# Down bias of all experts entered once, in the first pair's scatter, and a scatter that takes four banks in turn

## The chip, the cores and the metric

The kernel runs on one core of one Trainium2 chip. The metric is the device time of one execution in microseconds (us). Five engines matter here: TensorE (PE, with its weight loads listed apart as PEld), VectorE (DVE), ScalarE (ACT), GpSimd (POOL), and SyncE (SP), whose queue issues nearly all DMA transfers. The weights lie in HBM, the working memory is SBUF (`arena` in the profile), and TensorE writes its products to eight PSUM banks of 128 partitions x 512 float32 each.

## The reference, cut to what matters

One layer of a streaming encoder: RMSNorm, an input projection, two kinds of attention, an output projection, and then a mixture of 32 experts of which each token takes 4. 384 tokens (256 prompt rows, 128 sample rows) go through the experts. All is float32. The part that the change touches:

```python
logits = x2 @ w_router + b_router
top_val, top_idx = lax.top_k(logits, 4)
gates = softmax(top_val)
# for each expert e, for the tokens that chose it
hcat = x2[ids] @ w_gu[e] + b_gu[e]               # 1024 -> 2048
glu  = minimum(hcat[:, 0::2], 7)
lin  = clip(hcat[:, 1::2], -7, 7)
act  = glu * sigmoid(1.702 * glu) * (lin + 1)
out  = act @ w_dn[e] + b_dn[e]                   # 1024 -> 1024
y[token] += out * gate
```

The sum over experts of gate times `b_dn[e]` is linear in the bias, so it equals the matrix product of the gates (384 x 32, zero where an expert was not chosen) with `b_down` (32 x 1024).

## The kernel before, in words

The first 310 us hold norms, projections, attention, the router and the first gather. The rest is the experts, in 16 pairs (`pair`, called by `run_pairs` with `main`). The two experts of a pair have 64 slots each, so 128 rows together; expert 0 of a pair owns rows 0 to 63 and expert 1 rows 64 to 127. An expert's weights are read from HBM once, in pieces of 2 MB: a pair has 12 pieces, 8 of gate and up weights and 4 of down weights. They go through a ring of 8 buffers in SBUF. SP issues the load of a piece as soon as TensorE has done the piece that lay in its buffer (`refill`, line 575, waiting for `piece_done`); for the pieces numbered 8, 9, 16, 17, 28 and 29 it goes by halves (line 589). All pieces go in one order that is written out by hand.

TensorE's order within a pair:

1. Gate and up products (line 1943), 64 instructions of 64 columns by 512 to banks 0 to 3, with four products of 32 rows for the bias `b_gate_up` after the first eight (line 1929). They wait for their pieces.
2. If there is a next pair: its gather (line 1912), 24 products of 128 x 128 to banks 6 and 7, which ACT and DVE copy out (lines 1039 and 1444).
3. Two products of 32 rows that put the pair's `b_down` rows into banks 0 and 1 (line 1957, with `own_e`, a table of which row belongs to which expert, and `bdn2`, in which the left half of `b_down` lies on partitions 0 to 31 and the right half on 32 to 63). They wait until DVE has made two of the four parts of `act`, which empties banks 0 and 1. In the last pair a filler product follows (`keep_busy`, line 1788).
4. A wait for the six additions of the pair before (`y_added`), a wait for the last part of `act`, then eight transposes of `act` to banks 4 and 5 (line 1963) and three of the gated selection to bank 3 (line 1969).
5. Down products (line 1996; in the last pair also 1982) onto the bias in banks 0 and 1.
6. The scatter (line 2013): six products of 128 x 128 by 128 x 512, each adding its part of the pair's rows to a third of the tokens and half of the columns. It uses banks 4 and 5 in turn, and product n (from 2 on) waits for the addition of product n-2, which DVE does (line 1489). In the last pair six banks are used and nothing is waited for.

DVE makes the activation in four parts (lines 1471 to 1473 and 1459, with ACT's sigmoid at line 1045), then copies the next gather, the transposed activation and the result. `Y_BASE` and `at_` only turn counts into semaphore values. `GT` is the table of gates, 128 tokens x 32 experts for each of three groups of tokens; it is there since the router.

Of the kernel before, what the change touches and what calls it, by code (L numbers as in the profile page):

```python
# [91 lines left out]
def build(nc, io, out):  # L92
    ctx = ExitStack()
    with ctx:
# [108 lines left out]
        EG = at3(a0 + 12288 + 3 * P, E, TOPK)  # L203
        bgu4 = at(hn0, 512)
        bdn2 = at(hn0 + 512, 512)
        RK = at3(lf0, 3, E)
        GT = at3(lf0 + 96, 3, E)
        M = at3(lf0 + 192, 3, E)
# [141 lines left out]

        def scat_bank(n, last_one):

            return banks[(4, 5, 6, 7, 2, 3)[n] if last_one else 4 + n % 2]

        def turned_row(k):

# [433 lines left out]
        def _(ac):  # L790
# [248 lines left out]
                    nc.scalar.activation(XT[u][:, k], banks[6][:, P * k:P * (k + 1)], ACT.Copy,  # L1039
                                         scale=gcol_x[:, k:k + 1]).then_inc(xg_a, 1)  # L1040

            def pair(at_, u, next_at=None):
                for n in range(4):
                    ac.wait_ge(glu_ready, at_(4, n + 1))
                    nc.scalar.activation(sg[n % 2], tg[n % 2], ACT.Sigmoid, scale=1.702).then_inc(sig_ready, 1)  # L1045
                if next_at:
                    gathered(next_at, 1 - u)
                ac.wait_ge(actT_done, at_(2, 1))
                nc.scalar.activation(actT[:, 0:4], banks[4].rearrange("p (c s) -> p c s", c=4), ACT.Copy).then_inc(actT_a, 1)
                ac.wait_ge(selT_done, at_(1, 1))  # L1050
                nc.scalar.activation(gT, banks[3][:, 0:384], ACT.Copy).then_inc(selT_copied, 1)
                ac.wait_ge(down_done, at_(1, 1))
                nc.scalar.activation(rows[:, 0:512], banks[0], ACT.Copy).then_inc(rows_a, 1)  # L1053
# [1 line left out]
            ac.wait_ge(s_gx, 16)  # L1055
            gathered(lambda k, c: c, 0)
            gates(2)
            run_pairs(ac, lambda it, u, at_, nx: pair(at_, u, nx))

            def over(p, r, at_):  # L1060
                gathered(at_, 0)
# [449 lines left out]
        def _(pe):  # L1511
# [402 lines left out]
                    if k % 4 == 3:  # L1914
                        last.then_inc(xg_done, 1)

            def pair(at_, u, arrived, next_at=None, last_one=False, early=None):
                steps = [(k, n) for k in range(6) for n in range(4)]
                steps += [(6, 0), (6, 1), (7, 0), (7, 1), (6, 2), (7, 2), (6, 3), (7, 3)] if last_one else [(k, n) for n in range(4) for k in (6, 7)]
                slots_of = {}  # L1920
                for k, n in steps:
                    if (k, n) == (0, 0):
                        pe.wait_ge(xg_a, at_(4, 1))
                    if (k, n) == (1, 0):
                        pe.wait_ge(own_ready, at_(1, 1))
                        pe.wait_ge(s_bgu, 64)
                        for n_ in range(4):
                            grp = slice(E * n_, E * (n_ + 1))
                            mm(banks[n_], own_e[u][grp], bgu4[grp], start=False, stop=False, skip_group_check=True)  # L1929
                        pe.wait_ge(xg_a, at_(4, 4))  # L1930
                    if (k, n) == (4, 0):
                        pe.wait_ge(xg_v, at_(1, 1))
                    both = last_one and k >= 6
                    if both:
                        if n == 0:
                            slots_of[k] = arrived(k)
                        s = [slots_of[k]] * 2
                    elif k % 2 == 0 and n == 0:
                        s = [arrived(k + x) for x in range(2)]
                    for x in range(2):  # L1940
                        half = slice(SLOTS * x, SLOTS * (x + 1))
                        c0 = 2 * FF * (x if both else k % 2) + 512 * n
                        last = mm(banks[n][half], XT[u][:, k, half], piece_slot(s[x])[:, c0:c0 + 512],  # L1943
                                  start=(k == 0), stop=(k == 7), skip_group_check=True)
                        if n == 3 and (x == 1 if both else k % 2 == 1):
                            last.then_inc(piece_done, 1)
                        if (k, n) == (0, 3) and early == 0:
                            last.then_inc(half_done, 1)
                    if n < 3 and k == 7:
                        last.then_inc(h_done, 1)  # L1950
                if next_at:
                    gather(next_at, 1 - u)
                pe.wait_ge(act_ready, at_(4, 2))
                pe.wait_ge(s_bdn, 32)
                for hf in range(2):
                    grp = slice(E * hf, E * (hf + 1))
                    mm(banks[hf], own_e[u][grp], bdn2[grp], start=True, stop=False, skip_group_check=True)  # L1957
                if last_one:
                    keep_busy(banks[7], 512)
                pe.wait_ge(y_added, at_(6, Y_BASE))  # L1960
                pe.wait_ge(act_ready, at_(4, 4))
                for c in range(8):
                    last = nc.tensor.transpose(banks[4 + c // 4][:, P * (c % 4):P * (c % 4 + 1)],  # L1963
                                               act[:, P * c:P * (c + 1)], ident)
                    if c % 4 == 3:
                        last.then_inc(actT_done, 1)
                pe.wait_ge(selg_ready, at_(1, 1))
                for t in range(3):
                    last = nc.tensor.transpose(banks[3][:, P * t:P * (t + 1)], selg[u][:, t], ident)
                last.then_inc(selT_done, 1)  # L1970
                pe.wait_ge(actT_a, at_(1, 1))
                for i in range(3 if last_one else 2):
                    if i == 1:
                        pe.wait_ge(actT_v, at_(1, 1))
                    if last_one and i >= 1:
                        s = arrived(9 + i)
                        for hf in range(2):
                            for c in (2 * i - 2, 2 * i - 1):
                                for x in range(2):
                                    half = slice(SLOTS * x, SLOTS * (x + 1))  # L1980
                                    c0 = PIECE_W // 2 * x + D * (c % 2) + 512 * hf
                                    last = mm(banks[hf][half], actT[:, 4 + c, half], piece_slot(s)[:, c0:c0 + 512],
                                              start=False, stop=(c == 3), skip_group_check=True)
                            if i == 2 and hf == 0:
                                last.then_inc(down_done, 1)
                        last.then_inc(piece_done, 1)
                        continue
                    s = [arrived(8 + 2 * i + x) for x in range(2)]
                    order = [(hf, c) for hf in range(2) for c in range(4)]
                    if early is not None and i == 0:  # L1990
                        order = [(hf, c) for c in range(4) for hf in range(2)]
                    for hf, c in order:
                            for x in range(2):
                                half = slice(SLOTS * x, SLOTS * (x + 1))
                                w = piece_slot(s[x])[:, D * c + 512 * hf:D * c + 512 * (hf + 1)]
                                last = mm(banks[hf][half], actT[:, 4 * i + c, half], w, start=False,  # L1996
                                          stop=(i == 1 and c == 3), skip_group_check=True)
                                if (hf, c) == (1, 3):
                                    last.then_inc(piece_done, 1)
                                if early is not None and i == 0 and (hf, c) == (1, 1):  # L2000
                                    last.then_inc(half_done, 1)
                            if i == 1 and (hf, c) == (0, 3):
                                last.then_inc(down_done, 1)
                pe.wait_ge(selT_copied, at_(1, 1))
                for n in range(6):
                    t, hf = n // 2, n % 2
                    if n == 0:
                        pe.wait_ge(rows_a, at_(1, 1))
                    elif n == 1:
                        pe.wait_ge(rows_v, at_(1, 1))  # L2010
                    elif not last_one:
                        pe.wait_ge(y_added, at_(6, Y_BASE + n - 1))
                    mm(scat_bank(n, last_one), gT[:, P * t:P * (t + 1)], rows[:, 512 * hf:512 * hf + 512],  # L2013
                       start=True, stop=True).then_inc(scat_done, 1)

            def main(it, u, at_, nx):
                def arrived(r):
# [2 lines left out]
                    n = q if isinstance(it, int) and it == 0 else PIECES * PAIRS  # L2020
                    pe.wait_ge(ring_in[s], it * (16 * 3) + (16 * (q // RING + 1) + halved_in(s, n)))
                    return s
                pair(at_, u, arrived, nx, nx is None, early=u if isinstance(it, int) and it == 0 else None)

            run_pairs(pe, main, first_apart=True)

# [42 lines left out]
```

## Time and profile before

| | |
|---|---|
| runs shown | 1238.6, 1239.01, 1240.78 us; median 1239.01 us |
| span of the profiled execution | 1237.8 us |
| that execution's own device time | not listed apart; the span lies 1.2 us under the median |
| TensorE busy | 1205.1 us, 97% |
| VectorE, ScalarE, GpSimd busy | 350.3, 194.6, 158.6 us |
| mean granted TensorE clock | 0.996 |
| read from HBM | 442.00 MB |

The span runs from the first to the last instruction. "Busy" for TensorE holds the modelled time of pipelined products, so 97% does not say that it works at its peak. The clock is the share of full speed that was granted. The page cuts the span into 40 slices and gives the busy share of every engine in tenths for each.

### The profile page before, as it was taken

The page shows a single profiled execution, that of the slowest core. Times are in us where ns is not written, and L with a number is a line of the kernel's source. Part 1 is how long each engine was busy: PE and PEld are TensorE (multiplying, and loading weights), DVE is VectorE, ACT ScalarE, POOL GpSimd, SP SyncE. Part 2 cuts the span into 40 slices and gives each one's busy share as a digit, 9 for nine tenths or more (in the row PEclk, how much of TensorE's full clock was granted, in tenths as well). Part 3 has the DMA queues.
Part 4 walks back from the last instruction along what each step waited for, and adds up shares of the span by engine and source line. Part 5 has one row for each costly group of instructions (what it writes and reads, how often), then busy time and mean ns, then how long its engine had stood idle before and what let it go on. Part 6 is the DMA issues. An engine that isn't in the chain of part 4 may idle for free.

```text
span 1237.8 us, 16172 instructions
## 1 busy us (share of the span) xinstructions
PE 1205.1 (97%) x6101; PEld 525.3 (42%) x6102; DVE 350.3 (28%) x932; ACT 194.6 (16%) x519; POOL 158.6 (13%) x378
## 2 busy tenths in 40 slices
PE   9999999999999999999999999999999999999997
PEld 5444456646344343434343443434343434342433
DVE  3234366614322121213131222212121212131313
ACT  4211365513100010101010000101010101010100
POOL 0032312101320202012020202020202011020000
PEclk9999999999999999999999999999999999999999
DMA  9622343792999999999999999999999999999995
GB/s 299 258 67 98 139 138 141 272 406 94 387 425 421 426 427 427 427 428 430 428 429 427 428 430 426 430 427 430 428 428 430 426 430 426 429 430 426 428 425 225
DMA packets 57119, 448.66 MB, mean 362 GB/s; under 512 B 10594, under 2 KB 12019, under 8 KB 31219
## 3 DMA queue, kind: packets, MB, share of 16 engines
q1 hardware_dynamic: 57032, 448.05, 87.7%
q8 instruction: 29, 0.48, 0.2%
q14 instruction: 16, 0.12, 0.0%
q10 hardware_dynamic: 42, 0.01, 0.0%
HBM read 442.00 MB, written 4.86 MB: 361 GB/s over the span
## 4 chain that ended last, share of the span: by engine, by line
PE 75%; DMA 21%; DVE 2%; issue 1%; ACT 0%; SPq 0%; POOL 0%; DVEq 0%; POOLq 0%
DMA arena<-in_w_gate_up 21%; PE psum L1943 21%; PE psum L1996 17%; PE psum L1673 10%; PE psum L1912 7%; PE psum L1798 3%; PE psum L2013 3%; PE psum L1957 1%; PE psum L1963 1%; PE psum L1777 1%; PE psum L1709 1%; PE psum L1632 1%; PE psum L1929 1%; PE psum L1739 1%; PE psum L1623 1%
## 5 line engine op out<-in xcount | busy, mean ns | idle before, releaser
L1943 PE MATMUL psum<-arena 128*64 128x512 f32 x2048 | 451.9, 598 | 16.4 <-DMA arena<-in_w_gate_up 16.4
L1943 PEld LDWEIGHTS psum<-arena 128*64 128x64 f32 x2048 | 148.3, 138 | 315.4 <-issue 315.0
L1996 PE MATMUL psum<-arena 128*64 128x512 f32 x992 | 216.4, 594 | 0.7
L1471 DVE TENSOR_SCALAR arena<-psum 128x256 f32<-128x256 f32 x64 | 26.7, 418 | 394.3 <-PE psum L1943 394.3
L1996 PEld LDWEIGHTS psum<-arena 128*64 128x64 f32 x992 | 75.5, 137 | 130.7 <-issue 128.9
L1673 PE MATMUL psum<-arena 128*128 128x512 f32 x288 | 127.3, 595 | 1.4 <-DVE arena L1108 1.4
L1045 ACT ACTIVATE arena<-arena 128x256 f32<-128x256 f32 x64 | 26.7, 417 | 591.8 <-DVE arena L1471 591.8
L2013 PE MATMUL psum<-arena 128*128 128x512 f32 x192 | 92.8, 622 | 0.0
L743 POOL COPY arena<-arena 128x6 f32 (+1 forms) x16 | 3.0, 188 | 696.7 <-PE psum L1996 693.1
L1912 PEld LDWEIGHTS psum<-arena 128*128 128x128 f32 x720 | 81.5, 192 | 12.2 <-issue 12.2
L1912 PE MATMUL psum<-arena 128*128 128x128 f32 x720 | 84.4, 276 | 0.0
L1673 PEld LDWEIGHTS psum<-arena 128*128 128x128 f32 x288 | 53.4, 190 | 64.5 <-issue 62.5
L1489 DVE TENSOR_TENSOR arena<-psum,arena 128x512 f32<-128x512 f32 x96 | 66.5, 692 | 24.9 <-PE psum L2013 24.9
L1484 DVE COPY arena<-psum 128x512 f32<-128x512 f32 x16 | 11.1, 692 | 217.9 <-PE psum L1996 204.3
L2013 PEld LDWEIGHTS psum<-arena 128*128 128x128 f32 x192 | 28.9, 188 | 63.7 <-DVE arena L1489 39.5
L760 POOL TENSOR_SCALAR arena<-arena 128x64 f32<-128x64 f32 x96 | 53.9, 579 | 0.0
L1798 PE MATMUL psum<-arena 128*128 128x512 f32 x96 | 43.6, 599 | 1.0 <-DVE arena L1356 1.0
L1459 DVE TENSOR_TENSOR arena<-arena 128x256 f32<-128x256 f32 x64 | 36.4, 609 | 5.4
L751 POOL TENSOR_SCALAR arena<-arena 128x64 f32<-128x64 f32 x90 | 37.4, 440 | 0.0
L1053 ACT ACTIVATE arena<-psum 128x512 f32<-128x512 f32 x16 | 9.6, 598 | 162.4 <-PE psum L1996 150.6
L1444 DVE TENSOR_SCALAR arena<-psum,arena 128x128 f32<-128x128 f32 x64 | 18.0, 345 | 48.1 <-PE psum L1912 45.8
L1473 DVE SCALAR_TENSOR_TENSOR arena<-arena 128x256 f32<-128x256 f32 x64 | 27.3, 426 | 2.2
(264 smaller groups left out, 797.9 us busy)
## 6 DMA issues: line engine op xcount, KB each, us to landing
arena<-in_w_gate_up SPq DMA_DIRECT2D x124, 2048.0 KB, 24.9
arena<-in_w_down SPq DMA_DIRECT2D x62, 2048.0 KB, 22.2
arena<-in_w_in SPq DMA_DIRECT2D x5, 2048.0 KB, 14.2
arena<-in_w_gate_up SPq DMA_DIRECT2D x8, 1024.0 KB, 13.6
arena<-in_cache_fox_k SPq DMA_DIRECT2D x8, 512.0 KB, 3.4
arena<-in_cache_diff_k SPq DMA_DIRECT2D x8, 512.0 KB, 4.5
arena<-in_cache_fox_v SPq DMA_DIRECT2D x8, 512.0 KB, 4.8
arena<-in_cache_diff_v SPq DMA_DIRECT2D x8, 512.0 KB, 6.1
```

The costliest lines, as they stand in the source:

```text
L751: last = nc.gpsimd.tensor_scalar(sel[u][:, t, cols], places, pRK[u][:, t, x:x + 1], None, ALU.is_equal)
L760: last = nc.gpsimd.tensor_scalar(selg[u][:, t, cols], places, pRK[u][:, t, x:x + 1], pG[u][:, t, x:x + 1], ALU.is_equal, ALU.mult)
L1045: nc.scalar.activation(sg[n % 2], tg[n % 2], ACT.Sigmoid, scale=1.702).then_inc(sig_ready, 1)
L1459: nc.vector.tensor_tensor(act_rows[:, 32 * n:32 * (n + 1)], ta[n % 2].rearrange("s (p q) -> s p q", q=8), sg[n % 2].rearrange("s (p q) -> ...
L1473: lk(nc.vector.scalar_tensor_tensor(out=ta[n % 2], in0=tl[n % 2], scalar=1.0, in1=tg[n % 2], op0=ALU.add, op1=ALU.mult))
L1489: nc.vector.tensor_tensor(y[:, t, cols], scat_bank(n, last_one), y[:, t, cols], ALU.add).then_inc(y_added, 1)
L1673: last = mm(z_bank(u), hnT[:, k, r0:r0 + n], wv[:, k], start=(k == 0), stop=(k == 7))
L1798: last = mm(banks[4 + n % 2], oT[:, k, P * t:P * (t + 1)], wv[:, k % 2, 512 * hf:512 * hf + 512], start=(k == 0), stop=(k == 7))
L1912: last = mm(banks[6 + k // 4][:, P * (k % 4):P * (k % 4 + 1)], x2n[:, t, P * k:P * (k + 1)], sel[u][:, t], start=(t == 0), stop=(t == 2))
L1943: last = mm(banks[n][half], XT[u][:, k, half], piece_slot(s[x])[:, c0:c0 + 512], start=(k == 0), stop=(k == 7), skip_group_check=True)
L1996: last = mm(banks[hf][half], actT[:, 4 * i + c, half], w, start=False, stop=(i == 1 and c == 3), skip_group_check=True)
L2013: mm(scat_bank(n, last_one), gT[:, P * t:P * (t + 1)], rows[:, 512 * hf:512 * hf + 512], start=True, stop=True).then_inc(scat_done, 1)
```

## The change

Three things. The bias products of every pair (step 3 above) are gone, and the first down product of a bank starts its sum (`start=True`). In pair 0 alone, the gates of all experts are transposed with six products against the identity, to bank 2, copied by ACT to `GTT` (on partitions 0 to 31 and again on 32 to 63), and after every second product of the scatter two products of 32 rows add gates times `b_down` to its two banks. And the scatter goes through banks 4, 5, 6, 7 in turn instead of 4 and 5. For that the wait for the additions of the pair before moves ahead of the gather, product 2 of the scatter waits for the copies of the next gather out of banks 6 and 7, and products 4 and 5 wait for the additions of products 0 and 1.

```diff
+        GTT = at(hn0 + 1024, 384)
...
-            return banks[(4, 5, 6, 7, 2, 3)[n] if last_one else 4 + n % 2]
+            return banks[(4, 5, 6, 7, 2, 3)[n] if last_one else 4 + n % 4]
...
# ScalarE
                 ac.wait_ge(selT_done, at_(1, 1))
+                if with_bias:
+                    nc.scalar.activation(GTT[0:2 * E], banks[2][0:2 * E, 0:384], ACT.Copy)
                 nc.scalar.activation(gT, banks[3][:, 0:384], ACT.Copy).then_inc(selT_copied, 1)
...
# TensorE
+                pe.wait_ge(y_added, at_(6, Y_BASE))
                 if next_at:
                     gather(next_at, 1 - u)
-                pe.wait_ge(act_ready, at_(4, 2))
-                pe.wait_ge(s_bdn, 32)
-                for hf in range(2):
-                    grp = slice(E * hf, E * (hf + 1))
-                    mm(banks[hf], own_e[u][grp], bdn2[grp], start=True, stop=False, skip_group_check=True)
                 if last_one:
                     keep_busy(banks[7], 512)
-                pe.wait_ge(y_added, at_(6, Y_BASE))
                 pe.wait_ge(act_ready, at_(4, 4))
...
                     last = nc.tensor.transpose(banks[3][:, P * t:P * (t + 1)], selg[u][:, t], ident)
+                if with_bias:
+                    pe.wait_ge(gates_ready, 1)
+                    for t in range(3):
+                        for hf in range(2):
+                            last = mm(banks[2][E * hf:E * (hf + 1), P * t:P * (t + 1)], GT[:, t], ident,
+                                      start=True, stop=True)
                 last.then_inc(selT_done, 1)
...
-                                last = mm(banks[hf][half], actT[:, 4 * i + c, half], w, start=False,
+                                last = mm(banks[hf][half], actT[:, 4 * i + c, half], w, start=(i == 0 and c == 0),
                                           stop=(i == 1 and c == 3), skip_group_check=True)
...
-                    elif not last_one:
-                        pe.wait_ge(y_added, at_(6, Y_BASE + n - 1))
-                    mm(scat_bank(n, last_one), gT[:, P * t:P * (t + 1)], rows[:, 512 * hf:512 * hf + 512],
-                       start=True, stop=True).then_inc(scat_done, 1)
+                    elif n == 2 and next_at:
+                        pe.wait_ge(xg_a, next_at(4, 4))
+                        pe.wait_ge(xg_v, next_at(1, 1))
+                    elif n >= 4 and not last_one:
+                        pe.wait_ge(y_added, at_(6, Y_BASE + n - 3))
+                    last = mm(scat_bank(n, last_one), gT[:, P * t:P * (t + 1)], rows[:, 512 * hf:512 * hf + 512],
+                              start=True, stop=not with_bias, skip_group_check=with_bias)
+                    if not with_bias:
+                        last.then_inc(scat_done, 1)
+                    elif hf == 1:
+                        pe.wait_ge(s_bdn, 32)
+                        for x in range(2):
+                            grp = slice(E * x, E * (x + 1))
+                            mm(scat_bank(n - 1 + x, last_one), GTT[grp, P * t:P * (t + 1)], bdn2[grp],
+                               start=False, stop=True, skip_group_check=True).then_inc(scat_done, 1)
```

`with_bias` is true in pair 0 only. ACT's first two pairs are now written out apart from its loop, as TensorE's were before.

## Rows read from the trace of the kernel before

**Rows 1.** Page: busy shares, transfers by slice, DVE's additions (busy us, mean ns).
```profile
PE 1205.1 (97%) x6101; PEld 525.3 (42%) x6102; DVE 350.3 (28%) x932; ACT 194.6 (16%) x519; POOL 158.6 (13%) x378
...
GB/s 299 258 67 98 139 138 141 272 406 94 387 425 421 426 427 427 427 428 430 428 429 427 428 430 426 430 427 430 428 428 430 426 430 426 429 430 426 428 425 225
...
L1489 DVE TENSOR_TENSOR arena<-psum,arena 128x512 f32<-128x512 f32 x96 | 66.5, 692 | 24.9 <-PE psum L2013 24.9
```

**Rows 2.** Windows: stretch, its length, busy us (instructions) by engine, clock, DMA share, GB/s.
```profile
350.00:374.00 24.00, 24.00 (x102) 7.57 (x100) 4.84 (x7) 0.60 (x1) 6.75 (x17) 1.00 1.01 425
374.00:378.00 4.00, 4.00 (x22) 1.38 (x20) 0.00 (x0) 0.00 (x0) 0.00 (x0) 1.00 0.97 365
...
431.00:640.00 209.00, 208.78 (x1036) 86.51 (x1034) 48.41 (x105) 18.94 (x45) 23.52 (x62) 1.00 1.01 428
640.00:1140.00 500.00, 485.84 (x2332) 196.72 (x2328) 111.35 (x231) 41.45 (x93) 57.40 (x143) 1.00 1.01 428
```

**Rows 3.** Waits: line, waited for, us in total, times, longest.
```profile
PE psum L1943 <- DMA arena<-in_w_gate_up: 16.4, 9, 2.7
```

**Rows 4.** Chain that ended last, pair 0: start, us, what.
```profile
344.24 1.06 PE psum L1957 x4
345.30 1.02 PE psum L1963 x8
346.33 0.33 PE psum L1969 x3
346.65 13.88 PE psum L1996 x64
360.54 5.77 PE psum L2013 x12
366.31 3.58 PE psum L1943 x16
```

**Rows 5.** The chain again: starts of pairs, waits for weights, end of last pair.
```profile
422.76 3.58 PE psum L1943 x16
...
479.37 3.58 PE psum L1943 x16
...
672.33 7.09 PE psum L1943 x32
...
731.06 7.09 PE psum L1943 x32
...
907.32 8.78 PE psum L1943 x32
...
1226.42 5.37 PE psum L2013 x12
```

**Rows 6.** Timeline of SP's queue: start, us, what.
```profile
360.56 0.80 SPq L575 DMA_DIRECT2D arena<-in_w_gate_up  x2
374.57 7.67 SPq L575 DMA_DIRECT2D arena<-in_w_down  x4
...
431.20 7.75 SPq L575 DMA_DIRECT2D arena<-in_w_down  x4
```

**Rows 7.** Windows of half a microsecond behind that issue.
```profile
376.00:376.50 0.50, 0.50 (x4) 0.14 (x2) 0.00 (x0) 0.00 (x0) 0.00 (x0) 1.00 0.41 131
```

**Rows 8.** Chain: six products of 128x128 in two column halves, from the attention.
```profile
177.52 0.95 PE psum L1761 x12
```

**Rows 9.** Chain: four products of 32 rows between line 1943's.
```profile
369.89 1.07 PE psum L1929 x8
```

**Rows 10.** Timeline of the last pair: start, us, what, idle time before it.
```profile
1202.58 0.14 PEld L1943 LDWEIGHTS psum<-arena 128*64 128x64 f32 x2 [0.38 <-DMA arena<-in_w_gate_up]
...
1203.99 0.43 DVE L1471 TENSOR_SCALAR arena<-psum 128x256 f32<-128x256 f32 x1 [23.86 <-PE psum L1943]
...
1208.83 1.13 PE L1957 MATMUL psum<-arena 32*128 32x512 f32 x4 [0.60 <-DVE arena L1459]
1209.85 1.05 DVE L1459 TENSOR_TENSOR arena<-arena 128x256 f32<-128x256 f32 x2
...
1211.04 1.06 PE L1963 MATMUL psum<-arena 128*128 128x128 f32 x8
```

**Rows 11.** Windows around two waits for weights, columns as in Rows 2.
```profile
1021.00:1026.00 5.00, 2.92 (x16) 0.89 (x14) 0.00 (x0) 0.00 (x0) 0.00 (x0) 1.00 1.01 429
...
1138.00:1143.00 5.00, 2.30 (x13) 0.61 (x10) 0.00 (x0) 0.00 (x0) 0.00 (x0) 1.00 0.99 423
1142.70:1150.70 8.00, 7.71 (x28) 2.91 (x30) 3.36 (x9) 0.93 (x3) 0.00 (x0) 0.79 1.00 426
```

More of the change, by code:

```diff
@@ L1040, in gathered, with pair @@
                                          scale=gcol_x[:, k:k + 1]).then_inc(xg_a, 1)
-            def pair(at_, u, next_at=None):
+            def pair(at_, u, next_at=None, with_bias=False):
                 for n in range(4):
@@ L1057, in _ @@
             gates(2)
-            run_pairs(ac, lambda it, u, at_, nx: pair(at_, u, nx))
+            run_pairs(ac, lambda it, u, at_, nx: pair(at_, u, nx, isinstance(it, int) and it == 0 and u == 0),
+                      first_apart=True)
             def over(p, r, at_):
@@ L1915, in gather, with pair @@
                         last.then_inc(xg_done, 1)
-            def pair(at_, u, arrived, next_at=None, last_one=False, early=None):
+            def pair(at_, u, arrived, next_at=None, last_one=False, early=None, with_bias=False):
                 steps = [(k, n) for k in range(6) for n in range(4)]
@@ L2022, in arrived @@
                     return s
-                pair(at_, u, arrived, nx, nx is None, early=u if isinstance(it, int) and it == 0 else None)
+                pair(at_, u, arrived, nx, nx is None, early=u if isinstance(it, int) and it == 0 else None,
+                     with_bias=isinstance(it, int) and it == 0 and u == 0)
             run_pairs(pe, main, first_apart=True)
```

## The prediction

> **What bounds the kernel now.** I read the page first. TensorE is busy 97% of the span, which invites the thought that any product taken away is time gained. But the line of transfers under it stands at 425 to 430 GB/s in nearly every slice of the expert part [rows 1]. So there are two candidates, and averages can't choose. The windows can: 428 GB/s from 431 to 640 us and 428 again from 640 to 1140 [rows 2], that is, flat at one value both where TensorE works through and where it stands still. The list of waits says that it does stand still, 9 times and 16.4 us in all, always at the gate and up products and always for their weights [rows 3].
>
> The chain shows when. From pair 2 to pair 3 the start of the gate and up products moves by 479.37 - 422.76 = 56.6 us: TensorE's own pace. From 672.33 to 731.06, after the first and the second wait, it moves by 58.7 us [rows 5]. A pair reads 12 x 2.097 MB = 25.2 MB, and at 428 GB/s that is 58.8 us. So the stream of weights is the slower of the two. TensorE starts with a full ring of eight pieces, uses up that lead by 2.2 us a pair, and from pair 6 on waits. In this part work taken off TensorE turns into a longer wait and nothing else. What sets the end is when the stream of weights starts to run without a hole, its bytes, and what follows its last pieces.
>
> **Where the stream still has a hole.** SP issues piece after piece as TensorE frees the buffers. In pair 0 and early in pair 1 the queue is short. After the issue at 360.56 the next is at 374.57, when TensorE is through the first two pieces of pair 1 [rows 6]. Over 374 to 378 us the rate is 365 instead of 428 GB/s [rows 2], so (428 - 365) x 4 / 428 = 0.6 us of stream are lost; the half microsecond from 376.0 shows the bottom, 131 GB/s [rows 7]. The queue had just run empty. From there on nothing is missing: one pair later the issue at 431.20 [rows 6] falls in a stretch with no dip. Hence the rule for this change: each microsecond by which pair 1 starts later makes the hole at 376 us one microsecond longer, and everything behind it, up to the last piece, comes that much later. Starting it earlier can gain 0.6 us at most.
>
> **The change part by part, in pair 0.** Steps on TensorE's path between the end of pair 0's gather and the start of pair 1:
> - The two bias products go: -1.06 us [rows 4].
> - Six products that transpose the gates come, each 128 rows by 32 columns by 128, in two column groups. The nearest row is six products of that length in two column groups: 0.95 us [rows 8]. The down products behind them started at 346.65, without a gap behind the transposes (1.02 and 0.33 us) [rows 4]. With both edits they start at 344.24 + 1.02 + 0.33 + 0.95 = 346.54: -0.1 us for the two together.
> - The scatter loses its waits for DVE. It takes 5.77 us with two banks [rows 4] and 5.37 in the last pair, with six and no wait [rows 5]: -0.4. Four banks should do the same, since product 4 comes more than three product times (0.9 us each) after product 0, and an addition takes 0.69 [rows 1]. The new wait of product 2, for the copies of the gather out of banks 6 and 7, costs nothing: they are done before the down products, which take 13.88 us. The wait of the gather for the old additions costs nothing either: a whole set of gate and up products lies between.
> - Three times two bias products of 32 rows by 512 come, between full products. The nearest row is the very form that is removed: two in 1.06 us [rows 4], so 3.2. At such a change of shape the neighbours lose a little too: 16 products of line 1943 ahead of line 1929 take 3.58, where 32 take 7.09 or less. I take 1.15 each, 3.45 us. Bounds: four products of the same shape took 1.07 [rows 9], so two might take 0.53, 1.6 in all; and run as full products one after the other two take 2 x 0.9, 5.4 in all.
>
> Sum: -0.1 - 0.4 + 3.45 = +2.95 us, bounds +1.1 and +4.9. Pair 1 starts at about 369.3 instead of 366.31. ACT's additional copy lies under the down products. DVE's additions come in couples; the last ends within pair 1's gate products and nobody waits for it there.
>
> The Trainium skill ("TensorE: Matmul & The Clock Gate", Part 3, on packing small matmuls) says that products of 32 rows on different row groups run side by side, so that two would cost hardly more than one. By that rule the bias costs 1.6 us and the sum falls to the lower bound of +1.1. The rows speak against it for two products and for it for four.
>
> **The other pairs.** Each of pairs 1 to 14 saves 1.06 + 0.4 = 1.46 us on TensorE. That covers pair 1's lateness within two or three pairs and then turns into waiting: the waits begin about pair 5 and grow from some 2 to some 3.7 us (58.75 - 56.5 + 1.46). Gain at the end: none.
>
> **The last pair.** Its pieces 6 and 7 arrive split so that TensorE needs piece 7 later. Before, the weight load at 1202.58 waited 0.1 us for it [rows 10]: product stream and transfer met. The product followed at 1203.0 and DVE began at 1203.99. Now the piece comes 2.95 us later, at 1205.5, and TensorE, being early, stands there; after a wait a product starts about 0.1 us behind its data, so the products run from 1205.6 instead of 1203.0 + 2.95: -0.4. From there to the transposes DVE's four parts set the pace: last part done at 1209.85 + 1.05 = 1210.90, transposes at 1211.04 [rows 10]. Bias products and filler lay within that; taking the bias out gives 0.05 us. Everything behind is the same: transposes, down products, 5.37 us of scatter with six banks, stores.
>
> Total: +2.95 - 0.4 - 0.05 = **+2.5 us**. Span 1240.3; the profiled span lies 1.2 under the median, so 1241.5 us. With the bounds +0.65 to +4.45: 1239.7 to 1243.5.
>
> **Rivals.**
> - *The clock falls in the last pair* (+1.2 on top). Of the waits for weights, one of 2.08 us (2.92 busy in 5.00, to 1026) left the clock at 1.00, and one of 2.70 us, to 1143, was followed by a stretch at 0.79 [rows 11], a mean of 2.4 and 1.2 GHz; 32 records then took 8.78 instead of 7.09 us in another such pair, from 907.32 [rows 5]. Waits of 3.7 us will do this more often. In the middle it costs nothing, since it only eats the wait to come. In the last pair the wait is about 1.1 us if the pair before was slowed, and 2.8 if not; only in the second case does the clock fall where the end hangs on it. DVE's pace hides a part of the 1.7 us: I take 1.2. Result 1242.7. The same page of the Trainium skill (Part 1, on oscillation) says that an array kept waiting for a transfer drops to half rate and restarts there; the trace agrees in two of nine waits.
> - *The bias is nearly hidden.* The 32-row products run side by side or fill gaps, pair 1 is late by 1.1 us or less: +0.65, 1239.7. For it: four cost as much as two in the rows. Against it: the removed pair itself, measured at 1.06.
> - *TensorE is the bound after all* (the other side). Then 14 pairs give 14 x 1.46 = 20.4, the last 1.06, pair 0 costs 2.95: -18.5, 1220.5 us. The 97% speak for it, and the unexplained part of the 428 GB/s: if the rate rose once TensorE asked sooner, time would fall at once. It decides from the point at which the stream can beat 58.7 us a pair. Against it: the rate didn't rise during nine waits, with five pieces outstanding.
> - *The four banks don't bring their 0.4 us*: 1241.9, inside the forecast's own spread.
>
> **How the numbers follow.** Forecast 0.53, clock 0.21, hidden 0.20, TensorE-bound 0.04, and 0.02 for a mishap. 0.2% is 2.5 us, about what can be told from no change here, and the forecast sits on that edge: of its 0.53 I give 0.29 to above 1241.5 and 0.24 to below. Slower: 0.29 + 0.21 = 0.50. Faster: 0.04 and a sliver, 0.05. Same: the rest, 0.45. The range of 8 in 10 takes in the hidden bias with half a microsecond below it for the scatter of the runs, and the clock case with 1 above: 1238.9 to 1244.0.
>
> **What would show it.** In pair 0 the stretch from the first scatter product to pair 1 grows from 5.77 to about 8.8 us; SP's issue at 374.57 moves to about 377.5; the hole behind it grows from 0.6 to about 3.5 us; every later landing and the end move by that. The down products of pair 0 start within 0.2 us of where they did. Scatters of pairs 1 to 14 take about 5.4 us, and the waits for weights sum to 30 us or more. I am wrong if the issue moves and the stream's end doesn't, or if the rate in the middle changes.

## The result, and the profile after

| | before | after |
|---|---|---|
| median of 8 runs | 1239.29 us (1238.6 to 1241.07) | 1243.04 us (1240.67 to 1244.26) |
| ratio after / before | | 1.0026, 95% interval 1.0016 to 1.0036 |
| span of the profiled execution | 1237.8 us | 1242.5 us |
| TensorE busy | 1205.1 us | 1192.0 us |

Slower by 0.26%, about 3.2 us by the ratio (the medians lie 3.75 apart), with 13 us less work on TensorE. That contrast is the whole case.

The page after, in the lines that answer to [rows 1]: busy shares, transfers by slice, and DVE's additions.

```profile
PE 1192.0 (96%) x6061; PEld 531.2 (43%) x6062; DVE 348.6 (28%) x932; ACT 187.5 (15%) x514; POOL 159.3 (13%) x378
...
GB/s 299 256 48 116 138 139 138 261 411 93 383 425 386 423 428 428 427 429 428 428 428 429 427 428 429 429 428 429 427 428 429 429 427 428 429 430 427 426 427 224
...
L1493 DVE TENSOR_TENSOR arena<-psum,arena 128x512 f32<-128x512 f32 x96 | 66.2, 692 | 23.6 <-PE psum L2021 17.9
```

The reader is to look at the 13th slice: 386 GB/s where there was 421. All others behind it are as before. What happened there stands in the windows (columns as in [rows 2], which has the same stretches of before):

```profile
374.00:378.00 4.00, 4.00 (x24) 1.23 (x22) 0.00 (x0) 0.00 (x0) 0.00 (x0) 1.00 0.87 369
378.00:382.00 4.00, 4.00 (x22) 1.29 (x18) 0.00 (x0) 0.00 (x0) 0.00 (x0) 1.00 0.50 147
...
431.00:640.00 209.00, 203.63 (x1014) 87.18 (x1012) 48.03 (x105) 17.43 (x43) 20.34 (x51) 0.99 1.01 428
640.00:1140.00 500.00, 476.05 (x2302) 199.69 (x2300) 110.63 (x231) 36.63 (x89) 61.02 (x153) 0.99 1.01 428
```

(428 - 369) x 4 / 428 + (428 - 147) x 4 / 428 = 3.2 us of stream are lost from 374 to 382 us, against 0.6 before. The rate in the middle is 428, untouched. TensorE stands the longer (list of waits; line, waited for, us in total, times, longest; compare [rows 3]):

```profile
PE psum L1947 <- DMA arena<-in_w_gate_up: 33.1, 20, 2.7
```

The chain around pair 0, to be laid beside [rows 4] (start, us, what). Line 1962 is the transposes, 1973 the transposed gates, 2001 the down products, 2021 the scatter, 2029 the bias products in it, 1947 the gate products of pair 1:

```profile
346.25 0.87 PE psum L1962 x8
347.13 0.33 PE psum L1968 x3
347.46 0.78 PE psum L1973 x12
348.23 13.88 PE psum L2001 x64
362.12 1.95 PE psum L2021 x4
364.06 1.06 PE psum L2029 x4
365.12 1.92 PE psum L2021 x4
367.04 1.06 PE psum L2029 x4
368.10 1.92 PE psum L2021 x4
370.01 1.06 PE psum L2029 x4
371.07 3.59 PE psum L1947 x16
```

And SP's issues (timeline), for [rows 6]:

```profile
362.14 0.80 SPq L576 DMA_DIRECT2D arena<-in_w_gate_up  x2
379.33 7.67 SPq L576 DMA_DIRECT2D arena<-in_w_down  x4
```

One thing must be taken out before starts are compared. The first gate product of pair 0 starts at 311.86 us after and at 309.85 before, though nothing ahead of it was changed. Most of those 2.0 us lie in the first 20 us of the span. The chain has one group of 16 projection products there, in the kernel before and in the one after:

```profile
10.01 7.10 PE psum L1673 x16
```

```profile
10.28 8.80 PE psum L1677 x16
```

The same work, behind the same idle time of 1.41 us. From 10 to 18 us the mean granted clock is 1.00 before and 0.79 after, so a part of it ran at the lower level. The ten profiles of this case put pair 0's first product either between 309.5 and 309.9 us or between 311.3 and 312.2, five of each. Three of the late ones (the changed kernel and two of its four variants) have the 8.80 us group. The other two, both variants of the kernel before, have the group at 7.11 and 7.13 and lose 1.6 us near 252 us, in 24 records that take 1.58 and 1.66 us instead of 0.99 and 16 that take 8.06 and 7.97 instead of 7.06, again with a lower clock (0.86 and 0.87 over 253 to 261 us). I take it for a toss from one execution to the next; with one profile of each kernel that is argued and not shown. So below I use a stretch that leaves it out: from the first gate product of pair 0 to the first scatter product of the last pair. Its two ends in the chain, before (the later end is in [rows 5]) and after:

```profile
309.85 3.58 PE psum L1943 x16
```

```profile
311.86 3.58 PE psum L1947 x16
...
1231.36 5.37 PE psum L2021 x12
```

| | from | to | stretch | against before |
|---|---|---|---|---|
| before | 309.85 | 1226.42 | 916.57 us | |
| after | 311.86 | 1231.36 | 919.50 us | +2.93 |

Of the 4.7 us between the two spans 2.0 lie ahead of the experts and 2.9 within them; what follows the last scatter's start is 0.2 shorter (for comparison, the timed ratio 1.0026 and its interval are 3.2 us, 2.0 to 4.5).

### The profile page after: what moved, and what is told of

The parts are those of the page before. It is cut to its first block, busy times and chain, and to the rows that moved or that the text cites. A ratio compares the mean times of both kernels' runs of the same rounds, so it can differ in the third digit from the quotient of the medians.

```text
span 1242.5 us, 16028 instructions
## 1 busy us (share of the span) xinstructions
PE 1192.0 (96%) x6061; PEld 531.2 (43%) x6062; DVE 348.6 (28%) x932; ACT 187.5 (15%) x514; POOL 159.3 (13%) x378
## 4 chain that ended last, share of the span: by engine, by line
PE 68%; DMA 28%; DVE 1%; issue 1%; SPq 0%; ACT 0%; POOL 0%; DVEq 0%; POOLq 0%
DMA arena<-in_w_gate_up 26%; PE psum L2001 17%; PE psum L1947 16%; PE psum L1677 10%; PE psum L1916 7%; PE psum L1802 3%; PE psum L2021 2%; DMA arena<-in_w_down 2%; PE psum L1781 1%; PE psum L1962 1%; PE psum L1713 1%; PE psum L1636 1%; PE psum L1743 1%; PE psum L1627 1%; PE psum L1652 1%
## 5 line engine op out<-in xcount | busy, mean ns | idle before, releaser
L1947 PE MATMUL psum<-arena 128*64 128x512 f32 x2048 | 457.4, 601 | 33.1 <-DMA arena<-in_w_gate_up 33.1
L1947 PEld LDWEIGHTS psum<-arena 128*64 128x64 f32 x2048 | 152.3, 138 | 333.6 <-issue 331.6
L2001 PEld LDWEIGHTS psum<-arena 128*64 128x64 f32 x992 | 75.7, 137 | 130.9 <-issue 129.0
L1677 PE MATMUL psum<-arena 128*128 128x512 f32 x288 | 129.0, 602 | 1.4 <-DVE arena L1112 1.4
L2021 PE MATMUL psum<-arena 128*128 128x512 f32 x192 | 87.6, 603 | 0.0
L1916 PEld LDWEIGHTS psum<-arena 128*128 128x128 f32 x720 | 81.5, 192 | 12.2 <-issue 12.2
L1677 PEld LDWEIGHTS psum<-arena 128*128 128x128 f32 x288 | 53.9, 192 | 65.6 <-issue 63.6
L2021 PEld LDWEIGHTS psum<-arena 128*128 128x128 f32 x192 | 33.6, 189 | 53.6 <-issue 44.3
L1802 PE MATMUL psum<-arena 128*128 128x512 f32 x96 | 43.6, 599 | 1.0 <-DVE arena L1360 1.0
```

The source lines that it names most:

```text
L1677: last = mm(z_bank(u), hnT[:, k, r0:r0 + n], wv[:, k], start=(k == 0), stop=(k == 7))
L1802: last = mm(banks[4 + n % 2], oT[:, k, P * t:P * (t + 1)], wv[:, k % 2, 512 * hf:512 * hf + 512], start=(k == 0), stop=(k == 7))
L1916: last = mm(banks[6 + k // 4][:, P * (k % 4):P * (k % 4 + 1)], x2n[:, t, P * k:P * (k + 1)], sel[u][:, t], start=(t == 0), stop=(t == 2))
L2021: last = mm(scat_bank(n, last_one), gT[:, P * t:P * (t + 1)], rows[:, 512 * hf:512 * hf + 512], start=True, stop=not with_bias, skip_group ...
```

## The experiments

Each is told with its stretch, which leaves the toss out, and with its timed ratio to the kernel before where there is one. A stretch comes from one profile. Five of the eight agree with what was expected of them within 0.3 us and three miss by 0.8 to 1.0, so a difference of a few tenths between two of them is not resolved.

**Pure delay in pair 0.** The kernel before, with neither of the change's parts: three plain products behind pair 0's scatter, and in a second run six.

```diff
# kernel before, TensorE, behind pair(...)
+                if isinstance(it, int) and it == 0 and u == 0:
+                    for _ in range(3):
+                        mm(banks[2], ident, rows[:, 0:512], start=True, stop=True)
```

Expected, three products:

> The kernel before, with three further products of 128x128 by 128x512 (of no use to the result) at the end of pair 0's scatter, 0.9 us each, so 2.6 to 2.7 us. Measured from the first gate product of pair 0 to the first scatter product of the last pair, which is 916.6 us before (1226.42 - 309.85) and 919.5 after (1231.36 - 311.86). Theory H (the hole in the stream of weights): TensorE's delay there lengthens the hole behind the first refill of pair 1 one for one; the hole loses 3.2 us instead of 0.6, and the stretch becomes 919.2, +2.6. Rival A (absorbed): TensorE catches up in the later waits, stretch 916.6. Rival B (the bias products themselves, their shape or their writes onto a sum in progress, cost the time): no change here either, as these fillers are plain.

Measured: pair 0 longer by 2.57 us (59.03 instead of 56.46), stretch 919.25 (1230.76 - 311.51), +2.7; ratio 1.0017 (1.0003 to 1.0030). Its windows:

```profile
374.00:378.00 4.00, 4.00 (x24) 1.37 (x24) 0.00 (x0) 0.00 (x0) 0.00 (x0) 1.00 0.80 336
378.00:382.00 4.00, 4.00 (x20) 1.29 (x18) 0.00 (x0) 0.00 (x0) 0.00 (x0) 1.00 0.59 193
```

(92 + 235) x 4 / 428 = 3.1 us lost. Expected, six products:

> Twice the dose: six fillers at the end of pair 0's scatter. The stretch from pair 0's first gate product to the last pair's first scatter product was 916.6 before, 919.25 with three (pair 0 longer by 2.57). Theory H: +2.6 again, 921.8 (the work is in the hole, nothing absorbs it). Rival A (part of it is absorbed by the larger waits): 919.5 to 921.

Measured, in a single execution: pair 0 longer by 5.14 us, stretch 921.61 (1231.32 - 309.71), +5.04. The windows:

```profile
374.00:378.00 4.00, 4.00 (x24) 1.10 (x22) 0.00 (x0) 0.00 (x0) 0.00 (x0) 1.00 0.37 156
378.00:382.00 4.00, 4.00 (x22) 1.34 (x20) 0.00 (x0) 0.00 (x0) 0.00 (x0) 1.00 0.37 82
```

(272 + 346) x 4 / 428 = 5.8 us lost. The fillers in the chain, three and six (two records each):

```profile
367.96 2.58 PE psum L2026 x6
```

```profile
366.16 5.15 PE psum L2026 x12
```

Delay against stretch: 2.57 gives 2.7, 2.75 (the change) 2.93, 5.14 gives 5.04. One for one, and nothing special about bias products.

**More work elsewhere.** The same filler once in each of pairs 2 to 13.

```diff
# kernel before, TensorE, behind pair(...)
+                if not isinstance(it, int):
+                    for _ in range(1):
+                        mm(banks[2], ident, rows[:, 0:512], start=True, stop=True)
```

> The kernel before, with one such product after the scatter of each of pairs 2 to 13: 12 x 0.87 = 10.4 us more work for TensorE. Theory H: TensorE's pace becomes 57.4 us a pair, still under the stream's 58.7, so nothing: stretch 916.6 within 0.2, and the waits for weights fall from 16.4 to about 6 us. Rival A (TensorE is the bound, in part): up to +10.4, 927. Rival C (waiting costs, through the lower clock after long waits): fewer waits, so a little less time, down to -1.5.

Measured: stretch 917.40 (1227.13 - 309.73), +0.8; ratio 0.9989 (0.9977 to 1.0000). The waits:

```profile
PE psum L1943 <- DMA arena<-in_w_gate_up: 9.9, 10, 1.2
```

Ten microseconds of work cost at most eight tenths in the profile and nothing in the timed runs. TensorE isn't the bound. The waits fell by 6.5 us and not by the 10.4 that were added. Most of the rest is that the two stretches at the lower clock that follow waits in the kernel before (8.78 us instead of 7.09 for 32 records, 3.4 us together) are not there: all nine such groups take 7.09, and the longest wait is 1.2 us. So with shorter waits no slow stretch was seen, and the end gained nothing by it, against rival C. But 0.8 us is more than I had allowed. Its hole is the one of before (369 GB/s over 374 to 378). Behind it the rate is 428 over 431 to 640 and 640 to 1140 us, as before. The end is on the stream here too, with a wait of 0.31 us for a down piece in the last pair, which before doesn't have. I can't say whether the 0.8 is the fillers' or the scatter of one execution; one profile doesn't settle it.

**Four banks alone.**

```diff
# kernel before
-            return banks[(4, 5, 6, 7, 2, 3)[n] if last_one else 4 + n % 2]
+            return banks[(4, 5, 6, 7, 2, 3)[n] if last_one else 4 + n % 4]
# and, as in the change: y_added ahead of the gather, xg_a and xg_v at n == 2, y_added n - 3 from n == 4
```

> The kernel before, with the scatter in four banks and its waits alone, the bias of every pair where it was. Theory H: each scatter takes 5.4 instead of 5.8 us; pair 1 starts 0.4 us earlier, the hole shrinks by that, stretch 916.2, -0.4; the other 0.4s end in waits, which grow from 16.4 to about 21 us. Rival D (the earlier wait for the additions, or that for the next gather's copies, delays something): scatter or gather no shorter, stretch 916.6 or more.

Measured: pair 0's scatter 5.39 us, stretch 915.98 (1227.34 - 311.36), -0.6; waits 20.6 us; ratio 0.9993 (0.9980 to 1.0006). The four banks do what they say: the scatter is 0.4 us shorter and the waits grow by 4.2. The 0.6 at the end is in line with pair 0's 0.4, but with one profile it doesn't show it by itself.

**The bias in pair 3 instead of pair 0.**

```diff
# changed kernel; ACT and TensorE write out pairs 0 to 3
-                     with_bias=isinstance(it, int) and it == 0 and u == 0)
+                     with_bias=isinstance(it, int) and it == 1 and u == 1)
```

> The changed kernel, with the transposed gates and the bias products in pair 3 instead of pair 0 (pairs 2 and 3 are written out apart from the loops for it). Theory H: pair 1 starts 1.6 us earlier than before the change, the hole at the first refill of pair 1 closes (0.6 us), pair 4's refills have several us of queue ahead of them, and the stretch becomes 916.0 us, -0.6 against before and -3.5 against the change: about 1238.7 us. Rival B (the products cost wherever they are): 919.5, 1242.5 us. Rival C (more waiting means more stretches at the lower clock and costs at the end): 917 to 918.

Measured: stretch 916.24 (1226.13 - 309.89), -0.3 against before and -3.3 against the change; ratio 0.9993 (0.9981 to 1.0005), median 1238.91. No hole is left at 376 us:

```profile
374.00:378.00 4.00, 4.00 (x22) 1.32 (x20) 0.00 (x0) 0.00 (x0) 0.00 (x0) 1.00 0.98 418
378.00:382.00 4.00, 4.00 (x22) 1.41 (x20) 0.00 (x0) 0.00 (x0) 0.00 (x0) 1.00 1.02 434
```

The same products three pairs later cost nothing. TensorE's waits are 29.9 us here, nearly those of the changed kernel, and four groups of 32 records behind a wait ran slow, as there, so neither waiting nor the lower clock behind it is the price.

**The hole closed from the other side.** Bias products and late pair 1 stay; SP gets permission earlier.

```diff
# changed kernel
-HALVED = (8, 9, 16, 17, 28, 29)
+HALVED = (8, 9, 16, 17, 20, 21, 28, 29)
-                        if (k, n) == (0, 3) and early == 0:
+                        if (k, n) == (0, 3) and early is not None:
                             last.then_inc(half_done, 1)
```

> The changed kernel, bias products left in pair 0, but pieces 20 and 21 are loaded by halves: SP issues the first halves as soon as TensorE has done the first 2 x 1 MB of pair 1 (3.6 us after its start) instead of after 8.3 us. Pair 1 still starts 2.75 us late. Theory H: the issue comes at +3.6 and the stream has data 1.9 us later, about when its queue runs empty; the hole of 3.2 us shrinks to 0 there and to some 0.5 at the issue after it. Stretch 916.5 instead of 919.5. Rival B (the bias products or TensorE's lateness cost by themselves): 919.5.

Measured: pair 1 starts as late as in the changed kernel (59.21 us behind pair 0). SP's issue comes 3.6 us behind it and the rate holds (the starts of both pairs from the chain, then SP's issue, then the windows):

```profile
312.11 3.58 PE psum L1947 x16
...
371.32 3.58 PE psum L1947 x16
```

```profile
374.93 5.46 SPq L590 DMA_DIRECT2D arena<-in_w_down  x4
```

```profile
374.00:378.00 4.00, 4.00 (x24) 1.11 (x22) 0.00 (x0) 0.00 (x0) 0.00 (x0) 1.00 0.96 408
378.00:382.00 4.00, 4.00 (x22) 1.32 (x20) 0.00 (x0) 0.00 (x0) 0.00 (x0) 1.00 1.02 424
```

Stretch 916.36 (1228.47 - 312.11), ratio 0.9998 (0.9988 to 1.0009). The change's 2.9 us are gone while TensorE does exactly what it did. Together with the pure delay this shows the cause: not the work, but the refill that waits for it.

**Towards a better kernel.** Bias in pair 3 and halves at pieces 10, 11, 20 and 21:

```diff
# kernel with the bias in pair 3
-HALVED = (8, 9, 16, 17, 28, 29)
+HALVED = (8, 9, 10, 11, 16, 17, 20, 21, 28, 29)
-                        if (k, n) == (0, 3) and early == 0:
+                        if early is not None and ((k, n) == (0, 3) or early == 0 and (k, n) == (2, 3)):
```

> The kernel with the bias in pair 3 (stretch 916.24), and loads by halves also for pieces 10, 11, 20 and 21, so that the hole of 1.3 us at 324 to 328 us closes too. Theory H: everything behind comes 1.3 us earlier, stretch about 914.9, 1237.5 us. Rival A (holes this early are made up for by TensorE's lead or the ring): 916.2. Halves cost four more issues on SP at 0.4 us each, under its waits.

Measured: stretch 915.77 (1227.89 - 312.12), 0.5 better than with the bias in pair 3 alone and not 1.3, a miss by 0.9; ratio 0.9997 (0.9988 to 1.0006). The rates tell where the rest went. Over the first 10 us of pair 0 and the 12 us behind them the kernel with the bias in pair 3 alone has 369 and 378 GB/s (309.89 to 319.89 to 331.89 us), this one 352 and 414 (312.12 to 322.12 to 334.12). With 428 as the full rate the first lost 1.4 and 1.4 us there, the second 1.8 and 0.4. The hole that was meant closed by 1.0, and the one ahead of it was 0.4 larger. Together that is 0.6, beside a stretch shorter by 0.5. Whether the halves made the first hole larger isn't shown: the next kernel has the same halves, and its rates of 365 and 417 GB/s in these windows are 1.5 and 0.3 us lost. Rival A, made up for by the ring's lead, expected 916.2, and 0.5 us in one profile each doesn't refute it alone. Then the last pair:

```diff
# the same kernel; TensorE takes the last four pieces one by one
-                if q - PIECES in (6, 7, 10, 11):
+                if q - PIECES in (6, 7, 8, 9, 10, 11):
```

> The same, and in the last pair the down pieces 8 and 9 hold half the rows of both experts each, like 10 and 11, so that the first down products need piece 8 alone. In the changed kernel TensorE stood 0.38 us for piece 9 there (products at 1217.40, transposed activation ready about 1217.0). Theory H with this as the last link: stretch 0.4 us under the kernel beside it, 914.5. Rival E (the piece after it is late instead): no gain, 914.9.

Measured: stretch 915.50 (1225.05 - 309.55), ratio 0.9994 (0.9985 to 1.0003), median 1239.17; expected were 914.5, or 0.4 under the kernel beside it. The down products start without a wait, and TensorE then stands for the very last piece. The timeline of TensorE there (start, us, what, idle time before it):

```profile
1210.72 10.52 PE L1986 MATMUL psum<-arena 128*64 128x512 f32 x48
1221.39 3.65 PE L1986 MATMUL psum<-arena 128*64 128x512 f32 x16 [0.15 <-DMA arena<-in_w_down]
```

The stretch is 0.27 shorter, but most of that isn't the last pair's: from the first transpose to the first scatter product the last pair takes 15.68 us here (1225.05 - 1209.37) and 15.79 in the kernel beside it (1227.89 - 1212.10). The down products start 0.48 us earlier behind the transposes, and 0.1 of it is left at the scatter. That is nearly rival E. All four variants without the hole at 376 us have medians at or under the kernel before (by 0.03 to 0.9 us), none clear of noise; the ratio of each lies clearly under that of the changed kernel. Behind 330 us the stream of the last two has no hole to speak of. What none of these runs closed is the hole at the very first refill, in the first 10 us of pair 0: 1.4 to 1.8 us in the three kernels just told.

## Why the prediction was right, by its steps

**The bound.** Right. The two paces (56.6 us a pair for TensorE, 58.7 for the stream) told that work taken off TensorE would turn into waiting; the loop's pairs gave up 1.59 us each (480.96 - 425.94 = 55.02 from pair 2 to pair 3, instead of 56.61; I had 1.46, without the transposes told below), and they turned into waiting: the waits went from 16.4 to 33.1 us, and the rate in the middle stayed at 428 GB/s. The sentence that the end follows the last hole of the stream is what the fillers, the moved bias and the halves show from three sides.

**Pair 0.** Predicted +2.95 us, measured 59.21 - 56.46 = +2.75. The down products start 36.37 us behind the pair's first product instead of 36.80 [rows 4], -0.4 where I had -0.1, and so outside the 0.2 that I had named as a sign: the gates' products took 0.78, not 0.95, and the transposes run at 0.87 where a 32-row product no longer stands ahead of them (1.02). The scatter takes 8.95 instead of 5.77, +3.2 for a predicted +3.05. The bias products cost 1.06 each time, just like the form that was removed. The full products beside them take a little more too: each couple ahead of a bias product takes 1.92 to 1.95 us, where the six take 5.39 in the other pairs, 1.80 a couple. Together that is 1.19 each time, for the 1.15 that I took.

One reading of the prediction was wrong here, though no term of the sum hangs on it. The rule of the Trainium skill on packing ("TensorE: Matmul & The Clock Gate", Part 3) is that products on different row groups run side by side, so that two or four take little more than one. I made of it half of four's time, 0.53 us for two and 1.6 us in all, and said that the rows speak against it for two products. But two took 1.06 us and four 1.07 (line 1933), where one full product takes 0.9 in the scatter: the time hardly depends on how many, and the traces agree with the rule for both. The lower bound of +1.1 rested on that halving, which neither the rule nor a run supports.

**The stream.** Predicted one for one; the hole grew from 0.6 to 3.2 us, 2.6 for a delay of 2.75. SP's issue went from 374.57 to 379.33, +4.76, and +2.75 without the toss.

**The last pair.** Here a term failed in kind, though not in size that decides: I took 0.4 us off because TensorE would wait for piece 7 and start right behind it. It did. The timeline of the changed kernel's last pair, beside [rows 10]:

```profile
1207.52 5.37 PE L1947 MATMUL psum<-arena 128*64 128x512 f32 x24 [1.02 <-DMA arena<-in_w_gate_up]
1208.65 0.43 DVE L1475 TENSOR_SCALAR arena<-psum 128x256 f32<-128x256 f32 x1 [26.05 <-PE psum L1947]
...
1215.60 1.09 PE L1962 MATMUL psum<-arena 128*128 128x128 f32 x8 [1.65 <-DVE arena L1463]
...
1217.40 7.09 PE L2001 MATMUL psum<-arena 128*64 128x512 f32 x32 [0.38 <-DMA arena<-in_w_down]
```

The transposes start at 1215.60, 4.56 us later than before; without the 2.0 of the toss that is +2.55, as the forecast has it. But the down products start at 1217.40, 4.93 later: they stood 0.38 us for a down piece, the next in the stream. Before, that piece had come just in time. So the 0.4 were given back one link further on, and the end moved by +2.93, the stream's whole delay. I had asked what is late first and not what is late next.

**The total.** +2.5 forecast, +2.93 in the stretch, 3.2 timed with 2.0 to 4.5 around it. The median of 1243.04 lies 1.5 over the 1241.5. Of that 0.4 is the term just told, and 0.3 the median before, 1239.29 in these runs where I had started from 1239.01. The rest may be the toss of some 2 us ahead of the experts, for which the spans of the changed kernel's runs, 1238.9 to 1242.5, leave room. How often it falls badly in the timed runs of each kernel can't be seen from one profile each, so that part is argued and not shown.

**The rivals.** The lower clock in the last pair didn't come in the profiled run: TensorE stood there twice, for 0.72 and 1.02 us (predicted was one wait of about 1.1), as the pair before had been slowed (8.69 us for 32 records in the chain, from 1147.16). All in all such slow stretches came in four pairs (two before), and no cost of theirs at the end is seen. The hidden bias is refuted by the 1.06s, TensorE as the bound by its ten microseconds of filler, and the four banks did bring their 0.4 in the scatter.

```profile
1147.16 8.69 PE psum L1947 x32
```

## What to carry to other kernels

Where a ring of buffers feeds from a stream that runs at its limit, find the last moment at which the queue runs empty. Work ahead of that moment costs its full length at the end, even if it saves eight times as much in waits to come (here 14 pairs gave up 1.59 us each, and 2.75 were paid). Work behind it cost at most 0.8 us here, for 0.87 a pair with the two paces 2.2 apart, and nothing that can be seen for the bias once in pair 3; so a once-only cost belongs behind the hole. Then look at the stream's last pieces one after the other: the 0.4 us that were won at one of them were mostly waited for at the next.

## What the runs showed that I had not expected

The work ahead of the experts varies by 2 us between executions, through single stretches at the lower clock: 16 projection products at 10 us took 7.1 us in seven profiles and 8.80 in three, and 16 output products near 253 us took 7.06 before, and 8.06 and 7.97 in the profiles with three fillers and with four banks alone. With changes of 0.2% such a start is as large as the effect, and a stretch inside the profile agreed within 0.3 us with what was expected of it for five of the eight variants and missed by 0.8 to 1.0 for three, where the timed ratio of the change is known to 1.2 us either way.
